# Eight dense first keys instead of sixteen in the expert stage of a decoder layer

## The reference

```python
q = (xt @ w_q).reshape(n_tok, 8, 2, 128)
s = einsum('nhcd,hckd->nhck', q, sub_keys)          # 8 heads, 2 halves, 128 keys each
s1, i1 = top_k(s[:, :, 0], 16)
s2, i2 = top_k(s[:, :, 1], 16)
top_s, pos = top_k(all 256 sums s1 + s2, 16)
experts = (i1 * 128 + i2)[pos]                       # 16 of 16384 experts per token and head
gates = softmax(top_s)
h = gelu(einsum('td,thed->the', x, u_tab[experts]))
y = einsum('the,thed->td', gates * h, v_tab[experts])
```

## Time and profile before

| | |
|---|---|
| median of 3 runs | 1688.8 us (1682.46 to 1690.11) |
| profiled execution | 1687.17 us, its span 1685.4 us |
| busy share of the span | PE 92%, DVE 80%, ACT 29%, POOL 29% |
| moved by DMA | 571.57 MB, mean 339 GB/s |
| POOL's DMA queue (q0) | 450.03 MB, 65.8% of 16 engines' span |
| SP's DMA queue (q1) | 120.22 MB, 19.1% |

### The profile page before, as it was taken

How to read it: one execution, slowest core, us unless ns; L and a number is a source line. 1 busy time by engine, 2 the same in 40 slices (tenths; PEclk the granted TensorE clock), 3 DMA queues, 4 the chain that set the end, 5 groups by cost and what they waited for, 6 DMA issues and landing times.

```text
span 1685.4 us, 18487 instructions
## 1 busy us (share of the span) xinstructions
PE 1544.7 (92%) x6332; PEld 990.0 (59%) x6332; DVE 1342.7 (80%) x2260; ACT 495.4 (29%) x1142; POOL 484.9 (29%) x293
## 2 busy tenths in 40 slices
PE   9999999999898887988999889899898999998886
PEld 8999899888765554544555455355554444333332
DVE  4689999765877779888988899899998666655576
ACT  5433445733322222222222222322122212111121
POOL 0101011100132233343444434444344243323132
PEclk9999999999999999999999999999999999999998
DMA  6665544574899999998999999999999999999885
GB/s 247 198 234 191 186 165 149 202 276 151 359 420 427 427 426 428 423 380 341 366 389 390 362 377 393 407 411 390 372 404 406 375 413 403 394 410 389 332 326 225
DMA packets 58669, 571.57 MB, mean 339 GB/s; under 512 B 12969, under 2 KB 13641, under 8 KB 16713
## 3 DMA queue, kind: packets, MB, share of 16 engines
q0 software_dynamic: 39328, 450.03, 65.8%
q1 hardware_dynamic: 18580, 120.22, 19.1%
q10 hardware_dynamic: 672, 0.21, 0.1%
HBM read 665.68 MB, written 4.19 MB: 397 GB/s over the span
## 4 chain that ended last, share of the span: by engine, by line
DMA 40%; PE 26%; DVE 24%; issue 7%; ACT 2%; POOL 0%; SPq 0%; POOLq 0%; DVEq 0%; ACTq 0%
DMA uv_row<-in_uv_tab,eid 39%; PE psum L792 7%; DVE scratch L1626 7%; DVE scratch L1317 4%; PE psum L487 4%; PE psum L489 4%; PE psum L488 4%; DVE w_lo L1245 3%; PE psum L883 2%; DVE y_last L1635 2%; DMA w_raw<-in_w_stream 1%; DVE scratch L1646 1%; PE psum L733 1%; PE psum L813 1%; PE psum L617 1%
## 5 line engine op out<-in xcount | busy, mean ns | idle before, releaser
L792 PE MATMUL psum<-uv_row,scratch 128*128 128x512 f32 x1560 | 739.7, 612 | 117.9 <-ACT scratch L1151 117.5
L1626 DVE CUSTOM_DVE_ANT_0 scratch<-uv_row,x 128x2048 bf16<-128x2048 f32 x250 | 572.4, 2290 | 231.0 <-DMA uv_row<-in_uv_tab,eid 230.1
L455 POOL DMA_INDIRECT uv_row<-in_uv_tab,eid x254 | 443.6, 1746 | 778.2 <-DVE y_last L1635 437.0
L792 PEld LDWEIGHTS psum<-uv_row,scratch 128*128 128x128 f32 x1560 | 287.4, 192 | 464.3 <-issue 276.3
L1143 ACT ACTIVATE gel<-dots 128x1 f32<-128x1 f32 x256 | 51.8, 202 | 841.9 <-DVE dots L1626 841.8
L487 PE MATMUL psum<-xT_hi,w_hi 128*128 128x256 f32 x640 | 183.1, 286 | 2.9 <-DVE w_lo L1245 2.8
L1635 DVE SCALAR_TENSOR_TENSOR y_last<-uv_row,weight,y_last 128x512 f32<-128x512 f32 x240 | 179.7, 749 | 2.1 <-DVE popular L1585 0.2
L488 PE MATMUL psum<-xT_lo,w_hi 128*128 128x256 f32 x640 | 181.0, 283 | 0.0
L489 PE MATMUL psum<-xT_hi,w_lo 128*128 128x256 f32 x640 | 181.0, 283 | 0.0
L1245 DVE TENSOR_TENSOR w_lo<-w_raw,w_hi 128x2048 fp32r<-128x2048 f32 x62 | 141.7, 2286 | 29.4 <-ACT w_hi L942 28.5
L942 ACT ACTIVATE w_hi<-w_raw 128x2048 fp32r<-128x2048 f32 x62 | 118.8, 1916 | 85.3 <-DMA w_raw<-in_w_stream 85.2
(11 more groups left out here) (247 smaller groups left out, 1407.5 us busy)
## 6 DMA issues: line engine op xcount, KB each, us to landing
w_raw<-in_w_stream SPq DMA_DIRECT2D x63, 1024.0 KB, 4.8
dense_unit<-in_dense_u SPq DMA_DIRECT2D x16, 1024.0 KB, 11.2
dense_unit<-in_uv_tab SPq DMA_DIRECT2D x16, 1024.0 KB, 11.2
wq_first<-in_w_stream SPq DMA_DIRECT2D x8, 1024.0 KB, 11.6
wq_third<-in_w_stream SPq DMA_DIRECT2D x4, 1024.0 KB, 11.4
uv_row<-in_uv_tab,eid POOLq DMA_INDIRECT x254, 18.0
xT_raw<-in_xT SPq DMA_DIRECT2D x4, 512.0 KB, 5.6
turned_rows<-dist_row POOLq DMA_DIRECT2D x1, 2048.0 KB, 14.2
```

What stands on the lines that cost most here:

```text
L455: pool.indirect_dma_start(dst, None, tab, bass.IndirectOffsetOnAxis(ap=ids, axis=0), bounds_check=tab.shape[0] - 1, oob_is_err=False).then ...
L792: last = pe.matmul(bank(i, n), diag[k], row[k][:, D + n * 512:D + (n + 1) * 512], start=False, stop=True, skip_group_check=True)
L1626: dve.tensor_tensor_reduce(row[k][:, 0:D] if s < PLACES else product, row[k][:, 0:D], x1[:, s // SLOTS, :], 1.0, 0.0, ALU.mult, ALU.add, d ...
```

## The change

`DENSE` becomes 8. The U parts go to the steps 48 + floor(9 m / 4) for m = 0 to 31, that is 48 to 117; the V parts to every second step from 176, 176 to 238; the join stays at step 240. The tiles with a column per dense key that the search for 16 maxima fills stay 16 wide; the upper eight of `dense_key` are set to -1, so that they match no key. The chunks' comparisons, products and the mix handle 8 columns per token instead of 16. Slots whose first key was among the upper eight are gathered now.

```diff
-DENSE = 16
+DENSE = 8
 SKIP = PK * PK
-DENSE_SLOT = [LATER * PARTS + 9 * m // 8 for m in range(DENSE * PARTS)]
+DENSE_SLOT = [LATER * PARTS + 9 * m // 4 for m in range(DENSE * PARTS)]
...
 VALUES_AT = ROW2_AT + 1
-JOIN_AT = VALUES_AT + DENSE * PARTS
+VALUE_SLOT = [VALUES_AT + 2 * m for m in range(DENSE * PARTS)]
+JOIN_AT = VALUE_SLOT[-1] + 2
...
-        dense_key = sb("dense_key", [P, DENSE])
-        dense_key_i = sb("dense_key_i", [P, DENSE], U32)
-        dense_count = sb("dense_count", [P, DENSE])
+        dense_key = sb("dense_key", [P, TOP])
+        dense_key_i = sb("dense_key_i", [P, TOP], U32)
+        dense_count = sb("dense_count", [P, TOP])
...
-                if VALUES_AT <= s < VALUES_AT + DENSE * PARTS:
-                    v_dense((s - VALUES_AT) // PARTS, (s - VALUES_AT) % PARTS)
+                if s in VALUE_SLOT:
+                    v_dense(VALUE_SLOT.index(s) // PARTS, VALUE_SLOT.index(s) % PARTS)
...
-                dve.tensor_copy(dense_key[:, :], dense_key_i[:, :]).then_inc(chosen, 1)
+                dve.memset(dense_key[:, DENSE:TOP], -1.0)
+                dve.tensor_copy(dense_key[:, 0:DENSE], dense_key_i[:, 0:DENSE]).then_inc(chosen, 1)
...
-                                       dense_key[:, :].rearrange("p (o j) -> p o j", o=1).to_broadcast(square), ALU.is_equal))
+                                       dense_key[:, 0:DENSE].rearrange("p (o j) -> p o j", o=1).to_broadcast(square), ALU.is_equal))
```

## The result

The changed kernel takes 1716.8 us (median of 4 runs, 1716.0 to 1719.4) against 1686.6 for the kernel before beside it: a ratio of 1.0182, 95% interval 1.0163 to 1.0201, or +30 us. The profiled execution took 1716.6 us, its span 1714.8.

A forecast was written before the change was run, and what follows sets the result against it. The prediction took DMA to bound the kernel, mostly gathers in flight. Bytes of +106.7 - 13.3 - 40.8 = +52.6 us, less 20.2 of idle time filled, gave +32.4 us, 1721 us; forecast range 1708 to 1733, chance 0.52.

The forecast's parts named there:

- The counts: DMA queues: 2,771 more rows fetched and 16 fewer units, putting POOL's queue at 495.4 MB and SP's at 103.4.
- item 1: POOL's gathers: 2,771 more rows fetched at 38.5 ns each, +106.7 us.
- item 3: SP's 1 MB loads for dense keys: 16 fewer units at 2.55 us each, -40.8 us.
- item 2: POOL's gathers: 2,771 fewer skipped rows at 4.8 ns each, -13.3 us; bounds zero and double.
- item 4: Steps 48 to 239: 44.5 us of idle DMA time falls with the skipped share to 24.3, -20.2 us.
- The tail's 8.6 us: Steps after 239, DMA share 0.71: 256 of the added rows, 8.6 us, counted in full; bound, to lose them.
- items 5 and 6: Fewer matmuls on PE, smaller chunk operations on DVE and fewer ACT copies, all beside the DMA: counted at nothing.
- the bytes in full: Rival: idle DMA time stays because it comes from the loop's latency; +52.6 us, 1741; chance 0.20.
- all idle time filled: Rival: all idle DMA time is filled and the tail hides its share; 0 to +8 us, 1689 to 1697; chance 0.12.
- PE as the bound: Rival, V stage: PE at 4.29 us a step hides extra bytes; -55 us, 1634; chance 0.06, shared with an ineffective change.
- PE's clock: Rival, V stage: fewer matmuls lower PE's clock; about +10 us, 1731; above 1750, with longer landings, chance 0.04.
- Where it would grow: Largest growth in the short blocks: steps 64 to 79, which skipped most, and 128 to 143, without units.

The follow-up runs named there:

- none skipped: The changed kernel with the skip pattern empty, so every slot is fetched, also those of dense keys: 1790.0 us, ratio 1.0608 to the kernel before.
- the even eighth: The changed kernel, skipping the same 16 evenly spread partitions of 128 in every step from 48 on, 3,328 rows: 1664.3 us.
- the even patterns: Skipped rows from fixed, evenly spread partitions: on the changed kernel 1664.3 us; on the kernel before (16 keys, 6,032 rows) 1612.1 us, ratio 0.9559.
- the two engines: The changed kernel, skipping 3,328 rows, all on partitions 0 to 7 and 32 to 39: 1785.1 us, ratio 1.0579 to the kernel before.
- the mixed order: Same slots in another order of steps, heads mixed: kernel before 1660.9 us, ratio 0.9845; changed kernel 1702.1 us, ratio 1.0091.
- twelve keys: The changed kernel with DENSE = 12, its U and V parts respaced, join at 240: 1705.8 us, ratio 1.0113 to the kernel before.
- the run with the rows alone: The kernel before with slots of the upper eight keys gathered, still loading 16 + 16 units: 1757.7 us, ratio 1.0426.

## Why the prediction was right, point by point

The forecast was 1721 us, +32.4; measured 1716.8, +30.2.

- **The bound** (gathers in flight, DMA full): right. Every run followed the rows it fetched and how they lay on the engines.
- **The counts:** right to the last digit shown in both queues.
- **A row at 38.5 ns** (item 1): 37.8 by 3,328 rows, none skipped against the even eighth.
- **A unit at 2.55 us** (item 3): 2.56 by 16 units.
- **A skipped row at 4.8 ns** (item 2): wrong. A skipped row takes under 0.6 ns of wall time. The 2.9 us behind the term were longer packets of fetched rows, and these hardly went: over steps 48 to 239 what the rows' packets take above 616 ns is 35.1 us before and 31.1 after. With the small packets (4.9 to 3.5 us) that is -5.4 us, where the term has 2,515 x 4.8 = -12.1 for the same steps. That lies within the bounds that the forecast gave the term, but half of its relief wasn't there.
- **Idle time -20.2 us** (item 4): -16.9 by the same rows, -20.4 by the list of packets (43.9 to 23.5). The cause was right, shown by the even patterns, the two engines and the mixed order. So was the rule that idle time goes with the skipped share: by the list, it is 36.6 us with twelve keys, where the rule says 34.8, and 24.2 in the run with the rows alone. What doesn't go with the skipped share is the whole loss. Against its bytes at 38.5 ns a row and 2.55 us a unit, the stretch takes 84.6 us more with 16 keys and 57.9 with 8, a ratio of 0.68 and not 12.3 / 22.5 = 0.55, because the longer packets stay. (Against the even pattern it is 70.9 and 55.1, but with 16 keys that run is held up by DVE and PE.)
- **The tail's 8.6 us** (256 rows after step 239): mis-sized, +2.5 measured; the share there went from 0.71 to 0.76, so a good part of it was filled into idle time, about 3 us by these shares. The forecast named this bound and took the other end.
- In steps 48 to 239 the forecast was 52.6 - 8.6 - 20.2 = +23.8, measured +29.3, and item 2 is more than the difference. Too little there, too much in the tail, and 2.4 us ahead of step 48 that the change didn't make: the errors nearly cancel, and that the total is better than its parts is luck.
- **PE and DVE at nothing** (items 5 and 6): right, by the unit's price of 2.56 us with its matmuls gone.
- **The rivals:** the bytes in full and all idle time filled were both out, the idle time went to 0.54 of what it was by the list of packets, 0.62 by the shares. PE as the bound didn't occur in this change, but with 16 keys it is the bound of most of the V stage once the queues are even. PE's clock fell as feared, from 1.00 to 0.96 granted in the V stage, part of it at the lower of its levels of 1.2 and 2.4 GHz, and cost nothing visible: the even eighth has the same 0.96 there with the DMA engines full.
- **Where it would grow:** steps 64 to 79 (+5.7) and 128 to 143 (+6.6), as said; steps 112 to 127 as well (+7.3), which wasn't.

## What to carry to other kernels

A transfer that leaves out rows saves no more than its slowest DMA engine saves: count rows per engine over the window of buffers in flight, not in total, and order the work so that each engine's share is mixed. A mean DMA share of 0.96 can hide 8% of a stretch, because the loss shows partly as idle engines and partly as longer packets; the test is the same amount of skipping in an even pattern. Before a small remainder of a window is made the price of something, ask what else could take that time. And price both sides of a trade between "compute for all" and "fetch for some" in the one resource that is full: here 346 rows at 38 ns against a pair of units at 5.1 us, per key.

## What the runs showed of the hardware that was not expected

- A gather's rows are tied to DMA engines by destination partition: sparing two engines entirely gained 5 us of the 126 us that the same number of rows gains when spread.
- A row skipped as out of bounds costs next to nothing itself: it stays a packet of 4 bytes, 9 ns of one of 16 engines, and the even eighth leaves at most 1.5 ns of wall time for it.
- Among gathers with rows skipped by the data, a fetched row's packet of 16 KB takes 639 to 646 ns on average instead of 616. What lengthens it stays open.
- The page's line of HBM traffic counts skipped rows as read: POOL's queue moved 495.42 MB after the change and 549.47 MB with nothing skipped, yet the line is the same in both to 0.01 MB, and it doesn't show the rows that the change adds. The first line is of the kernel after, the second of the run with none skipped:

```profile
HBM read 648.90 MB, written 4.19 MB: 381 GB/s over the span
```
```profile
HBM read 648.91 MB, written 4.19 MB: 365 GB/s over the span
```
